# Second pair's cross attentions: unnormalised queries with the row factor in the softmax, memory products first, heads by halves, and an output turn held into the next product

## The reference, cut to what matters

```python
def rmsnorm(x, g):
    y = xf * lax.rsqrt(jnp.mean(xf * xf, axis=-1, keepdims=True) + EPS)
    return (y * g.astype(jnp.float32)).astype(x.dtype)
def cross_attn(hn, memn, wq, wk, wv, q_gain, k_gain, wo):
    q = rmsnorm((hn @ wq).reshape(bsz, t_len, C_HEADS, C_HEAD_DIM), q_gain)   # 4 heads of 256
    k = rmsnorm((memn @ wk).reshape(bsz, m_len, C_HEADS, C_HEAD_DIM), k_gain)
    v = (memn @ wv).reshape(bsz, m_len, C_HEADS, C_HEAD_DIM)
    logits = jnp.einsum('bthd,bmhd->bhtm', q, k).astype(jnp.float32) * C_HEAD_DIM ** -0.5
    p = jax.nn.softmax(logits, axis=-1).astype(v.dtype)
    o = jnp.einsum('bhtm,bmhd->bthd', p, v).reshape(bsz, t_len, D_MODEL)
    return o @ wo
```

## Time and profile before

| | |
|---|---|
| median of 3 runs | 3795.27 us (3793.78 to 3795.68) |
| the profiled execution, its own time | 3799.72 us |
| its span | 3797.9 us, 41533 instructions |
| busy PE | 3552.2 us (94%), 16790 matmuls |
| busy weight loads of PE | 2881.7 us (76%) |
| busy DVE | 1998.5 us (53%) |
| busy ACT | 1365.9 us (36%) |
| busy POOL | 390.9 us (10%) |
| mean granted TensorE clock | 0.965 |
| read from HBM | 308.75 MB, 82 GB/s over the span |

### The profile page before, as it was taken

One profiled execution on the slowest core, in us unless ns is written; L12 is line 12 of the kernel. 1 busy time (PEld: TensorE's weight loads), 2 busy tenths in 40 slices (PEclk: granted clock), 3 DMA queues, 4 the chain that ended last, 5 costly groups with the idle time before them and its releaser, 6 DMA issues.

```text
span 3797.9 us, 41533 instructions
## 1 busy us (share of the span) xinstructions
PE 3552.2 (94%) x16790; PEld 2881.7 (76%) x16790; DVE 1998.5 (53%) x3122; ACT 1365.9 (36%) x2230; POOL 390.9 (10%) x405
## 2 busy tenths in 40 slices
PE   8999999999999999999998888899999858889999
PEld 7767877888876787788887566778888736778887
DVE  4445366646554454665454875544333895554332
ACT  3333233424234333333333434434233444434231
POOL 1300110000041011000000010200000530200000
PEclk9999999999999999999998799999999979999999
DMA  3111232322221123222221012312322101312222
GB/s 141 61 34 62 95 129 83 106 95 94 89 95 45 51 78 127 96 99 96 94 98 61 30 63 82 111 46 99 100 95 89 67 17 65 104 67 89 98 96 78
DMA packets 88176, 315.64 MB, mean 83 GB/s; under 512 B 10544, under 2 KB 11824, under 8 KB 87472
## 3 DMA queue, kind: packets, MB, share of 16 engines
q1 hardware_dynamic: 87984, 312.98, 24.4%
HBM read 308.75 MB, written 4.19 MB: 82 GB/s over the span
## 4 chain that ended last, share of the span: by engine, by line
PE 74%; DVE 14%; issue 5%; POOL 4%; ACT 3%; DMA 0%; SPq 0%; DVEq 0%; ACTq 0%; POOLq 0%
PE bk L941 63%; PE bk L999 3%; PE bk L1035 3%; DVE ar L1912 3%; PE bk L1009 1%; DVE wl L1514 1%; POOL st L1997 1%; DVE wl L1508 1%; DVE al L1926 1%; POOL st L1995 1%; PE bk L955 1%; POOL x L2055 1%; DVE xl L1521 1%; DVE x L1537 1%; POOL ar L2092 0%
## 5 line engine op out<-in xcount | busy, mean ns | idle before, releaser
L941 PE MATMUL bk<-xh,wh 128*128 128x512 f32 (+1 forms) x2240 | 845.6, 378 | 19.9 <-DVE wl L1514 11.4
L1508 DVE TENSOR_TENSOR wl<-wr,wh 128x1024 fp32r<-128x1024 f32 x368 | 458.8, 1254 | 747.5 <-ACT wh L1176 746.7
L941 PE MATMUL bk<-xl,wh 128*128 128x512 f32 (+1 forms) x2240 | 841.1, 375 | 0.0
L941 PE MATMUL bk<-xh,wl 128*128 128x512 f32 (+1 forms) x2240 | 840.8, 375 | 0.0
L1176 ACT ACTIVATE wh<-wr 128x1024 fp32r<-128x1024 f32 x368 | 385.8, 1056 | 839.3 <-PE bk L941 774.8
L941 PEld LDWEIGHTS bk<-xh,wh 128*128 128x128 f32 x2240 | 424.9, 190 | 96.2 <-DVE wl L1514 12.6
L941 PEld LDWEIGHTS bk<-xh,wl 128*128 128x128 f32 x2240 | 424.3, 189 | 75.7
L941 PEld LDWEIGHTS bk<-xl,wh 128*128 128x128 f32 x2240 | 424.8, 190 | 74.0
L941 PE MATMUL bk<-wh,ah 128*128 128x512 f32 x1184 | 469.8, 397 | 8.8 <-DVE al L1957 5.0
L941 PE MATMUL bk<-wl,ah 128*128 128x512 f32 x1184 | 465.8, 393 | 0.0
L941 PE MATMUL bk<-wh,al 128*128 128x512 f32 x1184 | 465.8, 393 | 0.0
(11 more groups left out here) (248 smaller groups left out, 4283.6 us busy)
## 6 DMA issues: line engine op xcount, KB each, us to landing
wr<-in_wpk SPq DMA_DIRECT2D x544, 512.0 KB, 3.3
gb<-in_ln_g SPq DMA_DIRECT2D x6, 512.0 KB, 3.9
gb<-in_ln_b SPq DMA_DIRECT2D x6, 512.0 KB, 5.3
ar<-in_xT SPq DMA_DIRECT2D x4, 512.0 KB, 5.8
ar<-in_memT SPq DMA_DIRECT2D x2, 1024.0 KB, 4.8
x<-in_x SPq DMA_DIRECT2D x4, 512.0 KB, 4.8
park<-x SPq DMA_DIRECT2D x4, 512.0 KB, 6.1
x<-park SPq DMA_DIRECT2D x4, 512.0 KB, 5.2
```

The lines of the kernel that those rows point to most:

```text
L941: i = pe.e.matmul(dst, lw, rw, start=g not in opened, stop=end)
L1508: dve.e.tensor_tensor(m.wl[:, s, a], m.wr[:, r, a], m.wh[:, s, a].bitcast(F32), ALU.subtract) \
```

## The change

1. Queries (j = 2, 3) are no longer normalised before their transposes. `c_turn` waits for the raw copy. Tiles 0 and 2 are copied by DVE, 1 and 3 by ACT. ACT squares each head's 256 columns and sums them by its accumulator; POOL makes from it the root with the attention's scale in it (`c_rs`), and this column is the scale of Exp and a factor of the negated maximum.
2. Both gains are multiplied once per layer and applied to the keys as they leave PSUM (DVE); their row factor follows on DVE as before, POOL's multiplication is gone. Key squares are taken by ACT from PSUM, with the memory's row factor as scale.
3. Order: keys 0, keys 1, values 0 in one run of 12 units, with `rest` and the turns of the keys beside it (three steps between `c_norm` and the first turn; a turn of x for tile 2 or 3 is put off by a step), then queries 0, queries 1, values 1.
4. The attention C goes through heads 0 and 1 of all tiles, then 2 and 3.
5. `attend` with `hold` (X, M, C) stops two steps earlier; the last `oput` is kept in `held` and issued inside the next residual product, behind its first two outputs of unit 0. The first two units are then taken in the order written below.

```diff
-        self.items = [(t, q) for t in range(NT) for q in range(nh)]
+        group = group or nh
+        self.items = [(t, c * group + q) for c in range(nh // group) for t in range(NT) for q in range(group)]
...
+        if self.held:
+            steps[0:2] = [(0, outs[:2], None), ("held", None), (0, outs[2:-1], None), (1, outs[:-1], None),
+                          (0, outs[-1:], None), (1, outs[-1:], None)]
...
+            if s[0] == "held":
+                while self.held:
+                    self.held.pop(0)()
+                continue
...
+    def rests(self):
+        while self.rest:
+            if self.rest[0][0] == "turn" and self.rest[0][2] >= 2:
+                yield
+            self.step_rest()
+            yield
...
-        for i in range(n + 5):
+        for i in range(n + (3 if hold else 5)):
...
+        self.held = [f for _, f in later]
...
-        drive((self.attend(A, self.put(A)), 1))
+        drive((self.attend(A, self.put(A), True), 1))
...
+        def keys(j):
+            for t in range(2):
                 while got[j] <= t:
                     yield
                 self.add("c_norm", l, j, t)
+            for _ in range(3):
                 yield
-                g = self.take()
-                self.add("c_turn", l, j, t, g)
-                self.give(g)
+            for t in range(2):
+                turn(j, t)
+                yield
+
+        def queries(j):
+            for t in range(NT):
+                while got[j] <= t:
+                    yield
+                turn(j, t)
+                yield
...
+        def memory():
+            yield from proj(0, "cross_wk_2", 0, "mem", 2, gm)
+            yield from proj(1, "cross_wk_2", 1, "mem", 2, gm)
+            yield from values(0)
+        both = chain(lambda: keys(0), lambda: keys(1))
+        beside(memory(), (both, 1), (self.rests(), 1))
         self.turn_upto(NT)
-        drive((proj(2, "cross_wq_2", 0, "x", 4, gx), 1), (prologue(1, 2), 1))
-        drive((proj(3, "cross_wq_2", 1, "x", 4, gx), 1), (prologue(2, 4), 1))
-        drive((chain(lambda: values(0), lambda: values(1)), 2), (prologue(3, 4), 1))
-        A = Att(("C", l), si, 4, 256, 256, lambda t: (0, 2))
-        drive((self.attend(A, self.put(A)), 1))
+        drive((proj(2, "cross_wq_2", 0, "x", 4, gx), 1), (both, 1))
+        drive((proj(3, "cross_wq_2", 1, "x", 4, gx), 1), (queries(2), 1))
+        drive((values(1), 1), (queries(3), 1))
+        A = Att(("C", l), si, 4, 256, 256, lambda t: (0, 2), group=2)
+        drive((self.attend(A, self.put(A), True), 1))
...
-        pe.wait_ge(*ev["c_norm", l, j, t])
+        pe.wait_ge(*ev["c_norm" if j < 2 else "craw", l, j, t])
...
+        scale = m.crow(A, i) if A.name[0] == "C" else m.scale[A.name[0]]
...
+            on_act = j >= 2 and o % 2
+            if not on_act:
+                act.wait_ge(*ev["craw", l, j, o])
+            src = ps[:, :] if on_act or j < 2 else m.craws[j % 2][:, o, :]
...
+            for q in range(2):
+                a = slice(q * 256, q * 256 + 256)
+                i = act.e.activation(m.cq2[:, a], src[:, a], ACT.Square, bias=0.0, scale=scale, accum_out=ss[:, q:q + 1])
...
+            if on_act:
+                act.e.activation(m.craws[j % 2][:, o, :], ps[:, :], ACT.Copy) \
+                    .then_inc(*ev.up("act_ev", done, ("craw", l, j, o)))
...
+        if name == "C":
+            dve.wait_ge(*ev["c_rs", l, 2 + h // 2, t])
+            dve.e.scalar_tensor_tensor(nm, nm, -1.0, m.crow(A, i), ALU.mult, ALU.mult) \
+                .then_inc(*ev.up("dve_ev", ("nm", A.name, i)))
+            return
...
+            if j == 0 and o == 0:
+                for q in range(2):
+                    dve.wait_ge(*ev["d_gain", ("C", l), q])
+                dve.e.tensor_tensor(m.cgain[1], m.cgain[1], m.cgain[0], ALU.mult).then_inc(*ev.up("dve_ev"))
+                own()
...
+            dve.e.scalar_tensor_tensor(heads(m.craws[j][:, o, :], 2), heads(ps[:, :], 2), m.mrs[:, o:o + 1],
+                                       m.cgain[1].unsqueeze(1).broadcast_to([128, 2, 256]), ALU.mult, ALU.mult) \
...
+        if G.kind == "craw":
+            l, j = G.tag
+            ss = m.crms(j, o)
+            pool.wait_ge(*ev["c_sq", l, j, o])
+            rstd(ss, ss, *((1.0 / 256, RMS_EPS) if j < 2 else (1.0, 256 * RMS_EPS)), ("c_rs", l, j, o))
+            return
```

More of the change, by code:

```diff
@@ L134, with __init__ @@
 class Att:
-    def __init__(self, name, si, nh, dv, wide, keys):
+    def __init__(self, name, si, nh, dv, wide, keys, group=None):
         self.name, self.si, self.nh, self.dv, self.wide, self.keys = name, si, nh, dv, wide, keys
         self.per = 512 // dv
-        self.items = [(t, q) for t in range(NT) for q in range(nh)]
+        group = group or nh
+        self.items = [(t, c * group + q) for c in range(nh // group) for t in range(NT) for q in range(group)]
         self.no = {}
@@ L187, in __init__ @@
         self.split = self.rel = 0
-        self.rest = []
+        self.rest, self.held = [], []
         self.last_gate, self.last_branch, self.conv_g = {}, {}, None
@@ L319, in residual, with attend @@
             yield from self.gemm(G, None, tail=tail)
-    def attend(self, A, put):
+    def attend(self, A, put, hold=False):
         n = len(A.items)
         grp, later, no = {}, [], 0
-        for i in range(n + 5):
+        for i in range(n + (3 if hold else 5)):
             if i < n:
@@ L710, in prologue, with turn @@
                 self.add("c_norm", l, j, t)
+            for _ in range(3):
                 yield
-                g = self.take()
-                self.add("c_turn", l, j, t, g)
-                self.give(g)
+            for t in range(2):
[7 more added lines that the diff above has]
+                yield
+        def turn(j, t):
+            g = self.take()
+            self.add("c_turn", l, j, t, g)
+            self.give(g)
         def values(cg):
@@ L840, in slot, with crms, crow @@
         return self.u(12288 + 1024 * (t % 2), 1024) if si == 5 else self.gb[:, t % 2, :]
+    def crms(self, j, t):
+        a = 66 + 2 * (4 * j + t)
+        return self.st[:, a:a + 2]
+    def crow(self, A, i):
+        t, h = A.items[i]
+        return self.crms(2 + h // 2, t)[:, h % 2:h % 2 + 1]
     def gain(self, G, k):
@@ L1256, in qk @@
             act.wait_ge(*ev["p_turned", A.name, i - 3])
-        act.e.activation(pb, bk[sc.bank[g]][:, 0:(k1 - k0) * 128], ACT.Exp, bias=nm, scale=m.scale[A.name[0]],
-                         accum_out=sm).then_inc(*ev.up("act_ev", ("exp", A.name, i), ("free", g)))
+        scale = m.crow(A, i) if A.name[0] == "C" else m.scale[A.name[0]]
+        act.e.activation(pb, bk[sc.bank[g]][:, 0:(k1 - k0) * 128], ACT.Exp, bias=nm, scale=scale, accum_out=sm).then_inc(*ev.up("act_ev", ("exp", A.name, i), ("free", g)))
     def pt(A, i, g):
@@ L1370, in evac @@
                 .then_inc(*ev.up("act_ev", done, ("th", m0 + o)))
-        elif G.kind == "craw" and G.tag[1] >= 2:
+        elif G.kind == "craw":
             l, j = G.tag
-            act.e.activation(m.craws[j % 2][:, o, :], psum(g)[:, :], ACT.Copy) \
-                .then_inc(*ev.up("act_ev", done, ("craw", l, j, o)))
+            ps, ss = psum(g), m.crms(j, o)
+            if j < 2:
+                act.wait_ge(*ev["mrs", G.si])
+            scale = m.mrs[:, o:o + 1] if j < 2 else 1.0
+            on_act = j >= 2 and o % 2
+            if not on_act:
+                act.wait_ge(*ev["craw", l, j, o])
+            src = ps[:, :] if on_act or j < 2 else m.craws[j % 2][:, o, :]
+            if l or j or o:
+                act.wait_ge(*ev[("c_sq", l, j, o - 1) if o else ("c_sq", l, j - 1, 1 if j <= 2 else 3) if j else
+                                ("c_sq", l - 1, 3, 3)])
+            for q in range(2):
+                a = slice(q * 256, q * 256 + 256)
+                i = act.e.activation(m.cq2[:, a], src[:, a], ACT.Square, bias=0.0, scale=scale, accum_out=ss[:, q:q + 1])
+            if j < 2:
+                i.then_inc(*ev.up("act_ev", done, ("c_sq", l, j, o)))
+            else:
+                i.then_inc(*ev.up("act_ev", ("c_sq", l, j, o)))
+            if on_act:
+                act.e.activation(m.craws[j % 2][:, o, :], ps[:, :], ACT.Copy) \
+                    .then_inc(*ev.up("act_ev", done, ("craw", l, j, o)))
     def iq_turn(cg, t, g):
@@ L1960, in c_norm @@
     def c_norm(l, j, t):
-        a = 66 + 2 * (4 * j + t)
-        ss, raw = m.st[:, a:a + 2], heads(m.craws[j % 2][:, t, :], 2)
-        dve.wait_ge(*ev["c_sq", l, j, t])
-        dve.e.tensor_reduce(ss, heads(m.cq2, 2), AX.X, ALU.add).then_inc(*ev.up("dve_ev", ("c_red", l, j, t)))
+        raw = heads(m.craws[j][:, t, :], 2)
         dve.wait_ge(*ev["c_rs", l, j, t])
-        dve.e.tensor_tensor(raw, raw, ss.unsqueeze(2).broadcast_to([128, 2, 256]), ALU.mult) \
-            .then_inc(*ev.up("dve_ev", ("c_scaled", l, j, t)))
+        own()
```

(2 more changed lines are left out.)

33 lines of the change are left out of this document (7 added, 26 removed).

## The result

| | before | after | ratio (95%) |
|---|---|---|---|
| median | 3795.47 us (3793.78 to 3795.72, 4 runs) | 3742.51 us (3740.92 to 3743.60, 4 runs) | 0.9861 (0.9844 to 0.9878) |
| the profiled execution, its own time | 3799.72 us | 3742.15 us | |
| its span | 3797.9 us | 3740.4 us | |

The change is 53.0 us faster in medians and 57.5 in spans. The forecast was 3747, range 3737 to 3763.

The account below looks back on a forecast made before the run. PE's matmul stream bounds it (74% of the chain). POOL waits 37.6, turn of x 2.2, held turns 4.4, clock 13.0, less 8.8 at keys and 0.2 for Exp: 48.2 us off 3795.27, giving 3747; range 3737 to 3763.

Parts of the forecast that it names:

- own case: Whole kernel: 48.2 us gained, to 3747 us, good to plus or minus 5; chance 0.45.
- rival E: Order drains as before; only the queries' 12.3 us per layer and the clock behind them come: 3762 us; chance 0.03.
- Queries unnormalised: Query turns in the cross attentions: all POOL waits except the keys' go, 12.3 us per layer.
- The walk at the keys: First key turn, l = 0: step-by-step engine times giving a 2.2 us stall against 6.04, then 0.5 at the second pair.
- The clock: PE's slow stretches after six stalls cost about 13 us; one of 1.7 us per layer should stay at the keys.
- The hold: Last output turn behind 12 residual matmuls: minus 2.7 us for two C, 1.7 for two X; M zero.
- Exp with a column: Softmax of the cross attention: column scale costs 0.09 us more per pass; 0.1 charged per layer, 0.2 in all.
- Zeros: Parts forecast to cost nothing, among them memory products first and heads by halves in the cross attention.
- A: Rival: the keys come in time, 8.8 us more gained, 3738 us; chance 0.22.
- B: Rival: the keys are as late as now, 20 us stay instead of 8.8, 3758 us; chance 0.20.
- C: Rival: ACT's queue is late at the query tiles, 10 us come back, 3757 us; chance 0.08.
- D: Rival: twelve memory units outrun the weight path, with waits for `wl`; slower, to 3803 us; chance 0.02.

Follow-up runs that it names:

- The arithmetic alone: Kernel before with the new arithmetic but the old order of products, turns and output turns: 3755.83 us, ratio 0.9897.
- experiment 9: Changed kernel with key turns later, gain product on POOL, and key products taken from PSUM one unit later, behind the next weight split: 3733.90 us, ratio 0.9839.
- experiment 10: The changed kernel run again, unaltered: 3742.28 us, ratio 0.9857.
- experiment 6: Changed kernel with tiles outermost in the cross attention, as before the change: 3740.98 us, ratio 0.9855.
- experiment 7: Changed kernel with both halves of the values behind the queries: 3742.95 us, ratio 0.9859.
- Experiment 5: Changed kernel with two steps instead of three between the keys' norm and their turns: 3753.34 us, a single run.
- order-alone kernel: Kernel before's arithmetic with the new order and held turn, query norms one step ahead of their turns: 3789.22 us, ratio 0.9983.

## Why the prediction was right, point by point

*The direction, the size and the range* held: own case 3747, measured 3742.5. Against the two profiled executions the forecast gain was 48.2, the measured one 57.5. C and X with the stages behind it, which the sum was about, gave 54.0: 52.3 against 46.5 forecast in C, 1.7 against 1.7 in X. The rest, 3.5, is M, convolution and the other stages, for which nothing was forecast. Without it the gain would still be larger than forecast, by 5.8. The range leaves less out than its sentence says: rival E's 3762 lies inside it.

*Queries unnormalised.* Right. The arithmetic alone removes every query wait. Both sides of the sum are as forecast, 12.3 per layer, and the clock stretches behind them go too.

*The walk at the keys.* Right, in its instants and not only in its result, once all of its times are moved by one number. The turn of x for tile 0, which stands in front of the walk and is not touched, comes 3.09 us earlier in the trace of after, because the stages before it are shorter. First the line of before, then those of the kernel after:

```profile
2352.86 1.03 PE L955 MATMUL bk<-cst,gb 128*128 128x128 f32 x8
```

```profile
2349.77 1.03 PE L996 MATMUL bk<-cst,gb 128*128 128x128 f32 x8
...
2361.26 0.68 DVE L1759 TENSOR_TENSOR x<-x,bk 128x512 f32<-128x512 f32 x1
...
2367.26 0.68 DVE L1759 TENSOR_TENSOR x<-x,bk 128x512 f32<-128x512 f32 x1
...
2393.41 0.63 PE L1183 MATMUL bk<-cst,ar 128*128 128x128 f32 x4 [0.29 <-DVE ar L2032]
```

I had tile 2's residual sum at 2364.35 and tile 3's at 2370.35, less 3.09 that is 2361.26 and 2367.26, where they stand. DVE was to be done with the weight split at 2376.35, moved 2373.26, and the gain product starts there (experiment 9's first fence). The transposes were due at 2380.7, moved 2377.61, and start at 2377.51. PE was due at 2378.47, moved 2375.38, and came at 2375.76. Its seven units are there too: one, four and two, with a turn of x behind the first and behind the fifth. The 0.1 and the 0.4 make the stall 1.75 for 2.2. At the second pair the moved walk has 2393.51 and PE at 2393.16, so 0.35 and not the 0.5 that I wrote; the trace has 2393.41 and 0.29.

*The clock.* This is the mis-sized term. I wrote "A stall of 2.2 should still cost one slow stretch", 1.7 us per layer, 3.4 in all. No such stretch came in C in any of the eight traces whose longest stall there was about 1.75 or less. The trace of before had only stalls of 4.59 and more in front of its slow stretches, so it could not show what a short one costs, and I took the dear end. What a stall of 2.2 itself costs no run shows. The whole 13.0 came, and 1.5 more: C lost 52.3, of which the waits of PE make 37.8 (18.5 and 19.3), and the clock with the refilling of the pipeline 14.5. I had 9.6 there.

*The hold.* Right: 4.8 net for 4.4. C gave 1.5 for 1.34. X gave 1.3 for 0.85, but the longer stretch at 0.5 behind it takes 0.5 of that back. I had not thought of this cost, and that X comes out at its 0.85 is luck. M was forecast at zero plus or minus 0.7; inside its stage it lost 0.2 to 0.4, and what its clock did is open (experiment 10).

*Exp with a column.* The same Exp of 128x256 took 0.47; in the kernel after the source view of L1299 gives

```profile
L1299 ACT ACTIVATE ar<-bk,st x16: 563/563/565, 2454.2 to 2483.8; 128x256 f32<-128x256 f32 x16
```

0.090 us more, as the forecast had it from the 1024-wide pass. Little of it is on the path: behind the last Exp of each attention the wait at L1076 grew from 0.58 to 0.77, and at l = 1 there is a new one of 0.16 at L1050. That is 0.5 in all against 0.2 charged. The Trainium skill, ScalarE: Activation LUTs, What ACT_TABLE_LOAD costs, gives 93 ns for the operand, and this row agrees; taken on all 32 Exps it would have been 2.9 us, of which 0.5 showed.

*Zeros.* Heads by halves (experiment 6) bring and cost nothing. Of the memory products in front, values 0 cost 0.5 per layer (experiment 7), by the second key pair's wait above all. The gain product took 0.42 for the 0.4 estimated. Moved to POOL it gave 0.54 per layer: it is on the path of the keys, as the walk had it.

*The rivals.* A (keys in time) was priced 8.8 below my own case. Experiment 9 is that case, and it gave 4.8 in C, because 3.4 of the 8.8 were the slow stretches that never came. Experiment 5, with the turn one unit sooner, is the nearest to B: C is 13.7 longer there than in experiment 9, where B had 20. C, D and E fell: no query turn waits, there is no wait for `wl` between keys and queries in the kernel after, and the order came out as meant.

Of the signs I named for the changed profile two were off: the waits on DVE at the keys are two per layer (1.75 and 0.29), which the walk had and the list of signs did not, and PE's busy time fell by 15.9, not by about 10.

## What to carry to other kernels

A factor that is constant along a row can leave an operand's path and enter where the row is handled anyway (here Exp's scale); that was worth seven tenths of the gain, and the order of work gave the rest only together with it. Where two in-order engines feed each other, put the work that depends on nobody (the weight split) in front of the exchange, and what a third engine can do (the gain product) outside it: with the later turns this gave 2.4 us per layer. Price a stall with its clock stretch only if the trace shows stalls of that length followed by one; otherwise keep both ends. And read the stage behind the one you shortened: the held turn took 1.3 us out of each X, and the clock took 0.5 of it back in the next stage.

## What the runs showed of the hardware

The stalls of PE in C and the granted clock behind them. In the eight traces with stalls up to 1.75 only, it never fell. Behind each of the 14 stalls of 4.45 to 6.09 us it was at 0.5, for 3.1 to 6.1 us. Between them it went both ways. The windows of the order-alone kernel, each beginning with the turn that ended a stall of 2.93, 2.90, 2.74 and 2.77 us:

```profile
2378.53:2384.00 5.47, 5.42 (x31) 4.57 (x32) 4.52 (x6) 3.04 (x6) 2.57 (x3) 1.00 0.06 13
3240.28:3243.55 3.27, 3.27 (x14) 3.17 (x15) 2.32 (x3) 3.02 (x6) 2.38 (x3) 0.50 0.00 0
```

```profile
2461.24:2466.50 5.26, 4.96 (x16) 3.70 (x16) 2.35 (x3) 2.58 (x4) 1.79 (x3) 0.68 0.22 88
3323.61:3327.00 3.39, 3.39 (x16) 2.53 (x16) 0.69 (x1) 2.58 (x4) 0.72 (x2) 1.00 0.40 141
```

The first and the last stay at 1.00, the two between fall. So at this length the stall alone does not tell; what else does is open. One more, of 3.30, ran into the next stall too soon to be read.

The same program, run twice, has stages that differ by 0.8 to 1.5 us (both X, the start of the first block and one more), while C and M repeat within 0.2. That is as much as the smaller edits here are worth, and it is why they were read from their own stage.
